# A two-layer attention block on one Trainium2 core: the values of a pair of heads move one slot later, next to another pair's scores

## The chip, the cores and the metric

The kernel runs on one core of one Trainium2 chip. Its engines have their own instruction streams, synchronised by semaphores: TensorE (PE in the rows, PEld for its weight loads), VectorE (DVE), ScalarE (ACT), GpSimd (POOL) and SyncE (SP), which issues the weight loads from memory. The metric is the device time in microseconds, median of the runs; lower is better. All times are microseconds unless marked ns.

## The reference, cut to what matters

Two layers, 256 tokens, width 1024, everything in float32. Each layer has three attention branches of 8 heads, a gated merge of them, and a feed-forward part.

```
z = x @ w_in; (c_q, c_kv, ..., gate_logit) = split(z)
o_mla = softmax(causal(q @ k.T * scale)) @ v               # q, k: 64 + 32 = 96 wide
o_fox = softmax(causal(q @ k.T * scale + decay)) @ v       # 64 wide
o_dsa = softmax(top-64 of the indexer(q @ k.T * scale - slope * dist)) @ v   # 64 wide
gates  = sigmoid(gate_logit + b_gate)                      # 3 x 1024 a token
merged = sum over branches of gates * (o_branch @ w_branch)
x = layernorm(ALPHA * x + merged @ w_out)
x = layernorm(ALPHA * x + (gelu(conv(x @ w_up[gate])) * (x @ w_up[value])) @ w_down)
```

## The kernel before, in words

**Products.** Every product with a weight matrix is done in three matmuls on rounded parts: high x high, high x low, low x high (`product`, L628 to L630). ScalarE makes the high part of each weight panel of 128 x 2048 (`split_hi`, L1105), VectorE the low part (`split_lo`, L1434). Six raw panels and four high parts are in memory at once, so a split waits until the panel four before it was used (`panel_used`).

**Slots.** The 24 heads are 12 pairs: pairs 0 to 3 are FOX, 4 to 7 MLA, 8 to 11 DSA. The attention runs in slots s = 0 to LAST_SLOT, on every engine in an order written out by hand. In each of the first 24 slots TensorE runs one gate tile (`gate_tile`: 24 matmuls of 128 x 256, a tile of `gate_logit`). From slot 24 on it runs the branch projections instead (`branch_panel(q)`: four tiles of 12 matmuls; the first two ahead of the attention work of the slot, the last two behind it). Tiles are counted here from 0: tile u is tile u % 4 of panel u // 4. They go to three PSUM banks in turn, so tile u waits until VectorE has merged tile u - 3. Panel 4 is the first that reads the outputs of DSA, and waits for the low half of pair 11's output.

**One pair i**, before: scores in slot 2i+1 (`scores`, L913: for each of two token tiles two heads, 128 and 256 keys wide); row minima on VectorE in slot 2i+2 (`row_least`, L1566 and L1578) and exponentials on ScalarE (`softmax_exp`, L1179); normalising in slot 2i+3 on VectorE (`normalise`, L1585 and L1590) and, on TensorE, the transposes of the probabilities (`turn_probs`, L925). In slot 2i+4 VectorE copies the even head's (`probs_even_out`, L1596), ScalarE the odd head's (`probs_odd_out`, L1186), and TensorE runs the values (`values`, L942). In slot 2i+5 ScalarE takes the high half of the output out of PSUM (`outputs_hi`, L1191) and VectorE the low half (`outputs_lo`, L1602). There is one PSUM bank for the outputs and one buffer `pts` for the turned probabilities. `even_slot_pair(s, lag)` gives the pair whose lag fits slot s.

**Shapes on TensorE.** FOX and DSA scores use 64 rows of the array, the two heads side by side; MLA scores use 96 rows. Values use 64 columns for each of the two heads, side by side. Everything else near them is 128 x 128, or 128 x 96 for the transposes of MLA's heads (`head_operands`, L892 and L893).

**Merges.** Behind slot 23 VectorE multiplies each branch tile with its gate (`merge`, L1620), and GpSimd adds them up (L1931). In slot 24 `row_least` of pair 11 runs on VectorE ahead of the first merge.

Of the kernel before, what the change touches and what calls it, by code (L numbers as in the profile page):

```python
# [28 lines left out]
NT = T // P  # L29
# [35 lines left out]
OUT_AT = BR_AT + 2 * NB  # L65
# [14 lines left out]
SLOTS = NB * H  # L80
# [4 lines left out]
W_BRANCH = (1, 0, 2)  # L85


LAG_S, LAG_E, LAG_T, LAG_V = 1, 2, 3, 4
LAST_SLOT = 2 * (PAIRS - 1) + LAG_V
HEAD_ROWS = (HD, QK, HD)  # L90

# [46 lines left out]
def build_program(nc, x, positions, w_in, b_gate, b_forget, q_norm, kv_norm, w_uq, w_ukv, w_branch, w_out,  # L138
                  ln1_g, ln1_b, w_up, conv_w, conv_b, w_down, ln2_g, ln2_b, out):
    ctx = ExitStack()  # L140
    with ctx:
# [306 lines left out]
        def even_slot_pair(s, lag):  # L448

            i, odd = divmod(s - lag, 2)  # L450
            return [i] if not odd and 0 <= i < PAIRS else []
# [173 lines left out]
        def _(pe):  # L625
# [270 lines left out]
            def scores(l, i):  # L896

                b, j = divmod(i, 4)
                if i > 0:
                    pe.wait_ge(s_maxima_ready, at("maxima_ready", l, 2 * i))  # L900
                else:
                    pe.wait_ge(s_index_relu_ready, at("index_relu_ready", l, NT))
                if b == MLA:
                    pe.wait_ge(s_head_ready, at("head_ready", l, 2 * j + 2))
                for t in range(NT):
                    for a in range(2):
                        if b == MLA:
                            q, k = qks[0:QK, a, 0, :], qks[0:QK, a, 1, :]
                        elif b == FOX:
                            q, k = spread_rows(fq_t, a)[:, j, :], spread_rows(fk_t, a)[:, j, :]  # L910
                        else:
                            q, k = spread_rows(sq_t, a)[:, j, :], spread_rows(sk_t, a)
                        ins = pe.matmul(ps[:, B_S[a], SPAN[t]], q[:, P * t:P * t + P], k[:, 0:P * (t + 1)],  # L913
                                        start=True, stop=True)
                ins.then_inc(s_scores_ready, 1)
# [12 lines left out]
            def values(l, i):  # L928

                b, j = divmod(i, 4)  # L930
                pe.wait_ge(s_turned_even_ready, at("turned_even_ready", l, i + 1))
                pe.wait_ge(s_turned_odd_ready, at("turned_odd_ready", l, i + 1))
                if i > 0:
                    pe.wait_ge(s_outputs_lo_ready, at("outputs_lo_ready", l, i))
                for c, cols in ((0, slice(0, T)), (1, slice(T, 3 * P))):
                    for a in range(2):
                        h = 2 * j + a
                        if b == DSA:
                            v = z1[:, c, Z_SV:Z_SV + HD]
                        else:  # L940
                            v = (fv, v_tok)[b][:, c, HD * h:HD * h + HD]
                        ins = pe.matmul(ps[HD * a:HD * a + HD, B_O, P * c:T], v, pts[:, a, cols], start=c == 0, stop=c == 1)  # L942
                ins.then_inc(s_pair_output, 1)

            def branch_panel(l, q, tiles=range(4)):

                n, c = divmod(q, 2)
                whi, wlo = panel(l, BR_AT + q, 4, 512)
                if c == 0 and 0 in tiles:

                    pe.wait_ge(s_outputs_lo_ready, at("outputs_lo_ready", l, 4 * (n + 1)))
                for jj in tiles:
                    u = 8 * n + 4 * c + jj
                    if u < 2:
                        pe.wait_ge(s_gate_ready, at("gate_ready", l, SLOTS - 1 + u))
                    if u >= len(B_PROJ):

                        pe.wait_ge(s_proj_gated, at("proj_gated", l, u - len(B_PROJ) + 1))
                    dst = proj_psum(u)
                    for k in range(4):  # L960
                        cols = slice(P * jj, P * jj + P)
                        ins = product(dst, whi[:, k, cols], wlo[:, k, cols], *outputs(4 * n + k), k == 0, k == 3)
                    if jj < 3:
                        ins.then_inc(s_proj_product, 1)
                    else:
                        ins.then_inc(s_panel_used, 1)
# [46 lines left out]
            for l in range(DEPTH):  # L1013
# [37 lines left out]
                for s in range(LAST_SLOT + 1):  # L1051
                    if s < SLOTS:
                        gate_tile(l, s)
                    if H - 1 <= s < 2 * H - 1:
                        head_operands(l, s - H + 1)
                    if SLOTS <= s:
                        branch_panel(l, s - SLOTS, (0, 1))
                    for i in even_slot_pair(s, LAG_S):
                        scores(l, i)
                    for i in even_slot_pair(s, LAG_T):  # L1060
                        turn_probs(l, i)
                    for i in even_slot_pair(s, LAG_V):
                        values(l, i)
                    if SLOTS <= s:
                        branch_panel(l, s - SLOTS, (2, 3))
                for q in range(LAST_SLOT - SLOTS + 1, 2 * NB):
# [29 lines left out]
        def _(act):  # L1096
# [160 lines left out]
            for l in range(DEPTH):  # L1257
# [103 lines left out]
                    if SLOTS <= s:  # L1361
                        split_hi(l, BR_AT + s - SLOTS + 3)
                outputs_hi(l, PAIRS - 1)
                split_hi(l, OUT_AT)
                split_hi(l, OUT_AT + 1)
                merged_hi(l, 0)
                merged_hi(l, 1)
# [59 lines left out]
        def _(dve):  # L1427
# [296 lines left out]
            for l in range(DEPTH):  # L1724
# [66 lines left out]
                for s in range(LAST_SLOT + 1):  # L1791
                    for i in even_slot_pair(s, LAG_T + 1):
                        if i < PAIRS - 1:
                            probs_even_out(l, i)
                    for i in even_slot_pair(s, LAG_E):
                        row_least(l, i)
                    if s % 2 == 0 and s < SLOTS:
                        split_lo(l, GATE_AT + s // 2 + 2)
                    for i in even_slot_pair(s, LAG_E + 1):
                        if i < PAIRS - 1:  # L1800
                            normalise(l, i)
                    for i in even_slot_pair(s, LAG_V + 1):
                        outputs_lo(l, i)
                    if s == SLOTS:
                        merge(l, 0, (0, 1, 2))
                        normalise(l, PAIRS - 1)
                        merge(l, 0, (3,))
                    if s == SLOTS + 1:
                        merge(l, 1, (0, 1))
                        probs_even_out(l, PAIRS - 1)  # L1810
                        merge(l, 1, (2, 3))
                    if s == SLOTS + 2:
                        merge(l, 2)
                    if SLOTS - 1 <= s:
                        split_lo(l, BR_AT + s - SLOTS + 3)
                    if 2 <= s < 18:
                        take_eight(l, s - 2)
                    if s == 17:
                        selection(l)
                outputs_lo(l, PAIRS - 1)  # L1820
                merge(l, 3, (0, 1))
                split_lo(l, OUT_AT)
                merge(l, 3, (2, 3))
                merge(l, 4, (0, 1))
                split_lo(l, OUT_AT + 1)
# [125 lines left out]
```

## Time and profile before

| | |
|---|---|
| time, median of 3 runs | 870.39 us (870.2 to 870.74) |
| profiled execution, its own time | 869.66 us |
| its span | 867.9 us |
| TensorE busy | 850.6 us, 98% |
| VectorE, ScalarE, GpSimd busy | 70%, 54%, 11% |
| attention slots of layer 0, layer 1 | about 87 to 207 us, 512 to 632 us |

A row's start is counted from the start of the span. TensorE's matmuls are pipelined: one lasts about 0.28 us in the rows and the next starts 0.12 us after it, so what a matmul costs is read from start to start. The profile records a float32 matmul, such as those of scores and values, as two, so that the four of a block stand as x8.

### The profile page before, as it was taken

The numbers are of one execution on the slowest core, as the hardware profiler recorded it, in microseconds if no ns is written. First come the engines' busy times: TensorE is split into PE (matmuls) and PEld (weight loads), VectorE is DVE, ScalarE is ACT, GpSimd is POOL, SyncE is SP. The second block draws the span as 40 slices with busy tenths as digits, with TensorE's granted clock in tenths as the row PEclk, the third lists the DMA queues.
The fourth block names the chain that finished last, engine by engine and source line by source line (L and its number), as shares of the span: only waits on it lengthen the run. The fifth ranks groups of instructions, "written<-read, shape, count | busy, mean of one in ns | idle before, by whom it ended". The sixth has DMA issues, their size and how long they took to land.

```text
span 867.9 us, 15821 instructions
## 1 busy us (share of the span) xinstructions
PE 850.6 (98%) x6364; PEld 790.9 (91%) x6364; DVE 609.8 (70%) x1111; ACT 469.4 (54%) x726; POOL 94.3 (11%) x112
## 2 busy tenths in 40 slices
PE   6999999999999999999999999999999999999996
PEld 6899999989999999988889999998898999999885
DVE  5775777877786877665666558778778777666554
ACT  5556867554355555553437477675544465554430
POOL 1003800003500000000000055000071000000000
PEclk9999999999999999999999999999999999999998
DMA  9756443334677666465846664434366776664731
GB/s 305 215 171 210 147 146 99 117 127 148 193 194 198 191 195 194 159 213 180 266 120 166 186 203 133 141 104 125 119 193 179 194 212 187 185 188 135 242 132 48
DMA packets 176407, 148.86 MB, mean 172 GB/s; under 512 B 18156, under 2 KB 149840, under 8 KB 176336
## 3 DMA queue, kind: packets, MB, share of 16 engines
q1 hardware_dynamic: 171712, 143.08, 55.1%
q10 hardware_dynamic: 4624, 4.78, 1.9%
q8 instruction: 50, 0.82, 0.4%
q14 instruction: 21, 0.17, 0.1%
HBM read 146.53 MB, written 1.05 MB: 170 GB/s over the span
## 4 chain that ended last, share of the span: by engine, by line
PE 94%; DVE 2%; ACT 1%; DVEq 1%; DMA 1%; issue 0%; SPq 0%; ACTq 0%
PE ps L628 29%; PE ps L629 28%; PE ps L630 28%; PE ps L913 3%; PE ps L942 2%; PE ps L925 2%; PE ps L686 1%; ACT w_hi L1105 1%; DVEq L1569 1%; DMA raw<-w_in 1%; DVE w_lo L1434 1%; PE ps L892 0%; PE ps L861 0%; PE ps L893 0%; PE ps L879 0%
## 5 line engine op out<-in xcount | busy, mean ns | idle before, releaser
L1434 DVE TENSOR_TENSOR w_lo<-raw,w_hi 128x2048 fp32r<-128x2048 f32 (+3 forms) x142 | 304.0, 2143 | 116.7 <-ACT w_hi L1105 116.6
L628 PE MATMUL ps<-xt_hi,w_hi 128*128 128x256 f32 x1232 | 349.3, 284 | 0.4 <-ACT fq_t L1130 0.4
L629 PE MATMUL ps<-xt_lo,w_hi 128*128 128x256 f32 x1232 | 343.8, 279 | 0.0
L630 PE MATMUL ps<-xt_hi,w_lo 128*128 128x256 f32 x1232 | 343.6, 279 | 0.0
L1105 ACT ACTIVATE w_hi<-raw 128x2048 fp32r<-128x2048 f32 (+3 forms) x142 | 252.8, 1785 | 76.1 <-PE ps L630 70.1
L628 PEld LDWEIGHTS ps<-xt_hi,w_hi 128*128 128x128 f32 x1232 | 231.6, 188 | 5.7 <-issue 4.3
L629 PEld LDWEIGHTS ps<-xt_lo,w_hi 128*128 128x128 f32 x1232 | 231.7, 188 | 0.1
L630 PEld LDWEIGHTS ps<-xt_hi,w_lo 128*128 128x128 f32 x1232 | 231.6, 188 | 0.0
L628 PE MATMUL ps<-w_hi,ht_hi 128*128 128x512 f32 x176 | 68.6, 390 | 0.0
L630 PE MATMUL ps<-w_hi,ht_lo 128*128 128x512 f32 x176 | 68.5, 389 | 0.0
L1215 ACT ACTIVATE cv<-ps,vec_t 128x256 f32<-128x256 f32 x44 | 20.8, 473 | 88.2 <-PE ps L630 84.3
L629 PE MATMUL ps<-w_lo,ht_hi 128*128 128x512 f32 x176 | 68.5, 389 | 0.0
L1931 POOL TENSOR_TENSOR merged<-merged,gated 128x256 f32<-128x256 f32 x32 | 39.6, 1264 | 204.1 <-DVE gated L1620 203.8
L1179 ACT ACTIVATE prob<-prob,least 128x128 f32<-128x128 f32 x96 | 42.8, 447 | 21.3 <-DVE least L1578 21.3
L628 PE MATMUL ps<-w_hi,xt_hi 128*128 128x256 f32 (+2 forms) x144 | 46.4, 322 | 3.4 <-DVE w_lo L1732 2.0
L1668 DVE SCALAR_TENSOR_TENSOR cv<-ps,vec_t,cv 128x255 f32<-128x255 f32 x44 | 21.2, 481 | 36.3 <-ACT cv L1215 36.3
L629 PE MATMUL ps<-w_lo,xt_hi 128*128 128x256 f32 (+2 forms) x144 | 45.4, 315 | 0.0
L630 PE MATMUL ps<-w_hi,xt_lo 128*128 128x256 f32 (+2 forms) x144 | 45.4, 315 | 0.0
L629 PEld LDWEIGHTS ps<-w_lo,ht_hi 128*128 128x128 f32 x176 | 33.0, 188 | 6.8
L628 PEld LDWEIGHTS ps<-w_hi,ht_hi 128*128 128x128 f32 x176 | 33.0, 188 | 6.8
L630 PEld LDWEIGHTS ps<-w_hi,ht_lo 128*128 128x128 f32 x176 | 33.0, 188 | 6.8
L628 PE MATMUL ps<-ot_hi,w_hi 128*128 128x256 f32 x128 | 36.7, 287 | 0.9 <-DVE merged L1620 0.9
(226 smaller groups left out, 1248.7 us busy)
## 6 DMA issues: line engine op xcount, KB each, us to landing
raw<-ffn_w_up SPq DMA_DIRECT2D x88, 512.0 KB, 5.2
raw<-w_in SPq DMA_DIRECT2D x84, 512.0 KB, 4.8
raw<-ffn_w_down SPq DMA_DIRECT2D x32, 512.0 KB, 4.1
raw<-w_branch SPq DMA_DIRECT2D x24, 512.0 KB, 4.6
raw<-w_out SPq DMA_DIRECT2D x16, 512.0 KB, 4.3
raw<-ffn_w_down SPq DMA_DIRECT2D x24, 256.0 KB, 3.0
ln_g<-ln_g ACTq DMA_DIRECT2D x4, 512.0 KB, 3.6
ln_b<-ln_b ACTq DMA_DIRECT2D x4, 512.0 KB, 5.3
```

What stands on the lines that cost most here:

```text
L628: pe.matmul(dst, a_hi, b_hi, start=first, stop=False)
L629: pe.matmul(dst, a_hi, b_lo, start=False, stop=False)
L630: return pe.matmul(dst, a_lo, b_hi, start=False, stop=last)
L913: ins = pe.matmul(ps[:, B_S[a], SPAN[t]], q[:, P * t:P * t + P], k[:, 0:P * (t + 1)], start=True, stop=True)
L925: ins = pe.transpose(ps[:, B_PT[a], P * c:P * c + P], prob[:, i % 2, a, P * c:P * c + P], ident[:])
L942: ins = pe.matmul(ps[HD * a:HD * a + HD, B_O, P * c:T], v, pts[:, a, cols], start=c == 0, stop=c == 1)
L1105: ins = act.activation(panel_hi(l, p)[0:n, cols], panel_raw(l, p)[0:n, cols], ACT.Copy)
L1179: ins = act.activation(p, p, ACT.Exp, scale=-1.0, bias=least[:, i % 2, a, t:t + 1], accum_out=rsum[:, i % 2, a, t:t + 1])
L1215: act.activation(cv[:, buf, :], ps[:, B_UP[f % len(B_UP)], 0:T], ACT.Copy, scale=column(vec_t, V_CW + 2 * FT, f)).then_inc(s_conv_first_ta ...
L1434: ins = dve.tensor_tensor(panel_lo(l, p)[0:n, cols], panel_raw(l, p)[0:n, cols], panel_hi(l, p)[0:n, cols].bitcast(F32), ALU.subtract)
L1668: dve.scalar_tensor_tensor(cv[:, buf, 1:T], ps[:, B_UP[f % len(B_UP)], 0:T - 1], column(vec_t, V_CW + FT, f), cv[:, buf, 1:T], ALU.mult, A ...
L1931: pool.tensor_tensor(merged[:, u % KD, :], merged[:, u % KD, :], gated[:, u % NGATED, :], ALU.add).then_inc(s_merged_added, 1)
```

## The change

`LAG_V` goes from 4 to 5: the values of pair i run in slot 2i+5, and its outputs are taken out in slot 2i+6. Within a slot of TensorE the values move from behind `turn_probs` to ahead of `scores`. In the scores the token tile with 256 keys runs first. There is one slot more (LAST_SLOT 27), so one split and one half merge move from behind the loop into it.

```
-LAG_S, LAG_E, LAG_T, LAG_V = 1, 2, 3, 4
+LAG_S, LAG_E, LAG_T, LAG_V = 1, 2, 3, 5
...
-                for t in range(NT):
+                for t in reversed(range(NT)):
                     for a in range(2):
...
                         branch_panel(l, s - SLOTS, (0, 1))
+                    for i in even_slot_pair(s, LAG_V):
+                        values(l, i)
                     for i in even_slot_pair(s, LAG_S):
                         scores(l, i)
                     for i in even_slot_pair(s, LAG_T):
                         turn_probs(l, i)
-                    for i in even_slot_pair(s, LAG_V):
-                        values(l, i)
                     if SLOTS <= s:
                         branch_panel(l, s - SLOTS, (2, 3))
...
                 outputs_hi(l, PAIRS - 1)
-                split_hi(l, OUT_AT)
                 split_hi(l, OUT_AT + 1)
...
+                    if s == SLOTS + 3:
+                        merge(l, 3, (0, 1))
                     if SLOTS - 1 <= s:
                         split_lo(l, BR_AT + s - SLOTS + 3)
...
                 outputs_lo(l, PAIRS - 1)
-                merge(l, 3, (0, 1))
-                split_lo(l, OUT_AT)
                 merge(l, 3, (2, 3))
```

TensorE, before, at the end of gate tile 22 with the values of pair 9 behind it, and at the end of gate tile 23 with the scores of pair 11 and the transposes of pair 10 (`z1` is the tile that holds DSA's values):

```order
L630 MATMUL ps<-xt_hi,w_lo 128x256
L942 MATMUL ps<-pts,z 64x256 x2
L942 MATMUL ps<-pts,z 64x128 x2
L628 MATMUL ps<-xt_hi,w_hi 128x256
...
L630 MATMUL ps<-xt_hi,w_lo 128x256
L913 MATMUL ps<-sk_t,sq_t 128x128 x2
L913 MATMUL ps<-sk_t,sq_t 128x256 x2
L925 MATMUL ps<-ident,prob 128x128 x6
L628 MATMUL ps<-ot_hi,w_hi 128x256
```

The same place now:

```order
L630 MATMUL ps<-xt_hi,w_lo 128x256
L942 MATMUL ps<-pts,z 64x256 x2
L942 MATMUL ps<-pts,z 64x128 x2
L913 MATMUL ps<-sk_t,sq_t 128x256 x2
L913 MATMUL ps<-sk_t,sq_t 128x128 x2
L925 MATMUL ps<-ident,prob 128x128 x6
L628 MATMUL ps<-ot_hi,w_hi 128x256
```

The values stand behind gate tile 23 now, with no gate tile between them and the scores, and the 256-wide scores are first.

VectorE, before, in slots 24 and 25, from the end of the row minima of pair 11 (L1578) over the merges (L1620) to the copy of pair 11's probabilities:

```order
L1578 ISA prob,least<-prob,selm 128x256
L1578 ISA least 128x1
L1620 SCALAR_TENSOR_TENSOR merged<-gates_early,ps 128x256 x3
L1585 RECIPROCAL rinv<-rsum 128x4
...
L1620 SCALAR_TENSOR_TENSOR merged<-gates_early,ps 128x256
L1434 TENSOR_TENSOR w_lo<-raw,w_hi 128x2048
L1602 TENSOR_TENSOR ot_lo_last<-ps,ot_hi_last 128x256
L1620 SCALAR_TENSOR_TENSOR merged<-gates_late,ps 128x256 x2
L1596 COPY pts<-ps 128x384
```

The same place now (every line number behind L1364 is one lower):

```order
L1577 ISA prob,least<-prob,selm 128x256
L1577 ISA least 128x1
L1601 TENSOR_TENSOR ot_lo_last<-ps,ot_hi_last 128x256
L1619 SCALAR_TENSOR_TENSOR merged<-gates_early,ps 128x256 x3
L1584 RECIPROCAL rinv<-rsum 128x4
...
L1619 SCALAR_TENSOR_TENSOR merged<-gates_early,ps 128x256
L1433 TENSOR_TENSOR w_lo<-raw,w_hi 128x2048
L1619 SCALAR_TENSOR_TENSOR merged<-gates_late,ps 128x256 x2
L1595 COPY pts<-ps 128x384
```

The low half of an output (of pair 9) stands between the row minima and the first merge; before, pair 9's stood in slot 23, and the one shown above is pair 10's.

ScalarE, now, from the copy of the odd head of pair 10 over the four exponentials of pair 11 in slot 24:

```order
L1186 ACTIVATE pts<-ps 128x384
L1179 ACTIVATE prob,rsum<-prob,least 128x128
L1179 ACTIVATE prob,rsum<-prob,least 128x256
L1179 ACTIVATE prob,rsum<-prob,least 128x128
L1179 ACTIVATE prob,rsum<-prob,least 128x256
L1191 ACTIVATE ot_hi_last<-ps 128x256
L1105 ACTIVATE w_hi<-raw 128x2048 x2
```

The high half of pair 9's output (L1191) stands behind the exponentials; before, it stood in slot 23, ahead of the last gate.

## Rows read from the trace of the kernel before

**Rows 1.** The page: TensorE's and others' busy time; granted clock in 40 slices

```profile
PE 850.6 (98%) x6364; PEld 790.9 (91%) x6364; DVE 609.8 (70%) x1111; ACT 469.4 (54%) x726; POOL 94.3 (11%) x112
...
PEclk9999999999999999999999999999999999999998
```

**Rows 2.** Timeline of TensorE, slots 3 to 5: start, duration, engine, line, what [idle before]

```profile
99.41 0.28 PE L630 MATMUL ps<-xt_hi,w_lo 128*128 128x256 f32 x1
99.61 0.93 PE L913 MATMUL ps<-fk_t,fq_t 64*128 64x128 f32 x8
100.47 0.88 PE L925 MATMUL ps<-ident,prob 128*128 128x128 f32 x6
...
103.88 0.27 PE L630 MATMUL ps<-xt_hi,w_lo 128*128 128x256 f32 x1
104.08 0.87 PE L942 MATMUL ps<-pts,fv 128*64 128x256 f32 x8
104.88 0.38 PE L628 MATMUL ps<-xt_hi,w_hi 128*128 128x256 f32 x1
105.11 0.28 PE L629 MATMUL ps<-xt_lo,w_hi 128*128 128x256 f32 x1
105.22 0.28 PE L630 MATMUL ps<-xt_hi,w_lo 128*128 128x256 f32 x1
```

**Rows 3.** Timeline of TensorE, slot 9, scores of the first MLA pair

```profile
125.54 0.27 PE L893 MATMUL ps<-ident,k_tok 128*96 128x128 f32 x1
125.65 1.48 PE L913 MATMUL ps<-qks 96*128 96x128 f32 x8
126.96 0.82 PE L925 MATMUL ps<-ident,prob 128*128 128x128 f32 x6
```

**Rows 4.** Timeline of TensorE, slot 24 of layer 0: tiles 1, 2 and 3

```profile
191.32 0.28 PE L630 MATMUL ps<-ot_hi,w_lo 128*128 128x256 f32 x1
192.29 0.87 PE L942 MATMUL ps<-pts,z 128*64 128x256 f32 x8 [0.69 <-DVE pts L1596]
...
194.48 0.28 PE L630 MATMUL ps<-ot_hi,w_lo 128*128 128x256 f32 x1
195.26 0.38 PE L628 MATMUL ps<-ot_hi,w_hi 128*128 128x256 f32 x1 [0.50 <-DVE merged L1620]
```

**Rows 5.** Timeline of VectorE, slots 23 and 24 of layer 0

```profile
189.48 2.29 DVE L1434 TENSOR_TENSOR w_lo<-raw,w_hi 128x2048 fp32r<-128x2048 f32 x1 [2.41 <-ACT w_hi L1105]
191.68 0.55 DVE L1596 COPY pts<-ps 128x384 f32<-128x384 f32 x1
...
194.78 1.08 DVE L1620 SCALAR_TENSOR_TENSOR merged<-gates_early,ps 128x256 f32<-128x256 f32 x3
```

**Rows 6.** Timeline of ScalarE, slots 23 and 24 of layer 0

```profile
187.17 0.47 ACT L1163 ACTIVATE gates_late<-ps,bg 128x256 f32<-128x256 f32 x1 [2.16 <-PE ps L630]
...
195.65 0.19 ACT L1179 ACTIVATION_READ_ACCUMULATOR prob<-prob,least 128x1 f32 x1
195.74 1.90 ACT L1105 ACTIVATE w_hi<-raw 128x2048 fp32r<-128x2048 f32 x1
197.54 0.36 ACT L1191 ACTIVATE ot_hi_last<-ps 128x256 fp32r<-128x256 f32 x1
```

**Rows 7.** Timeline of VectorE, slot 19: low half of an output, behind pair 8's normalising

```profile
170.33 0.42 DVE L1602 TENSOR_TENSOR ot_lo<-ps,ot_hi 128x256 fp32r<-128x256 f32 x1
```

**Rows 8.** Timeline of TensorE, slot 19: first transpose of pair 8

```profile
171.37 0.33 PE L925 MATMUL ps<-ident,prob 128*128 128x128 f32 x1
```

**Rows 9.** Timeline of VectorE behind slot 26: a split while GpSimd adds

```profile
213.37 2.71 DVE L1434 TENSOR_TENSOR w_lo<-raw,w_hi 128x2048 fp32r<-128x2048 f32 x1
```

**Rows 10.** Timeline at the end: TensorE's last matmul

```profile
860.09 0.39 PE L630 MATMUL ps<-w_hi,ht_lo 128*128 128x512 f32 x1
```

**Rows 11.** Windows: stretch, its length, busy time (x) by engine, granted clock, DMA, GB/s

```profile
861.00:863.30 2.30, 0.00 (x0) 0.00 (x0) 1.98 (x6) 0.29 (x1) 0.00 (x0) 1.00 0.00 0
863.40:867.90 4.50, 0.00 (x0) 0.00 (x0) 2.01 (x3) 0.00 (x0) 0.00 (x0) 0.50 0.31 117
```

More of the change, by code:

```diff
@@ L85 @@
 W_BRANCH = (1, 0, 2)
-LAG_S, LAG_E, LAG_T, LAG_V = 1, 2, 3, 4
+LAG_S, LAG_E, LAG_T, LAG_V = 1, 2, 3, 5
 LAST_SLOT = 2 * (PAIRS - 1) + LAG_V
@@ L904, in scores @@
                     pe.wait_ge(s_head_ready, at("head_ready", l, 2 * j + 2))
-                for t in range(NT):
+                for t in reversed(range(NT)):
                     for a in range(2):
@@ L1057, in _ @@
                         branch_panel(l, s - SLOTS, (0, 1))
+                    for i in even_slot_pair(s, LAG_V):
+                        values(l, i)
                     for i in even_slot_pair(s, LAG_S):
@@ L1061, in _ @@
                         turn_probs(l, i)
-                    for i in even_slot_pair(s, LAG_V):
-                        values(l, i)
                     if SLOTS <= s:
@@ L1363, in _ @@
                 outputs_hi(l, PAIRS - 1)
-                split_hi(l, OUT_AT)
                 split_hi(l, OUT_AT + 1)
@@ L1813, in _ @@
                         merge(l, 2)
+                    if s == SLOTS + 3:
+                        merge(l, 3, (0, 1))
                     if SLOTS - 1 <= s:
@@ L1820, in _ @@
                 outputs_lo(l, PAIRS - 1)
-                merge(l, 3, (0, 1))
-                split_lo(l, OUT_AT)
                 merge(l, 3, (2, 3))
```

## Prediction

> **What bounds the kernel now.** I read the page's busy table first: TensorE is busy for 98% of the span and the clock row shows 9 in every slice but the last [rows 1]. Nothing can be gained here that doesn't shorten TensorE's own row of work or one of its waits, and any wait that is added is paid in full. Then I read TensorE's timeline over one pair of heads, and the chain of waits for the places where it stood still. In the slots of the attention there are none: for both layers TensorE's starts follow each other without a wait from the first scores to the end of slot 23. What is left there is the price of going from one kind of matmul to another.
>
> That price is read from start to start. Inside a gate tile matmuls start every 0.12 us (105.11 to 105.22). The first scores start 0.20 behind the last gate matmul (99.41 to 99.61), the first values too (103.88 to 104.08), and the first gate matmul behind the values takes 0.23 until the next may start (104.88 to 105.11) [rows 2]. So a gate tile that stands behind values and ahead of scores pays about 0.085 at its end and 0.11 at its start. The scores' block is 0.86 long and the values' 0.80. MLA's scores use 96 rows; they start 0.11 behind the transpose ahead of them and take 1.31 (125.65 to 126.96): no switch is paid [rows 3].
>
> The other place is slot 24, where branch tiles take the place of the gate tiles. TensorE waits there twice: the values of pair 10 wait for the copy of the turned probabilities on VectorE (0.69), and the fourth branch tile (tile 3; only three banks serve them) waits 0.50 for VectorE's first merge [rows 4]. Both hang on one chain: the end of gate tile 23 frees the last gate on ScalarE (187.17) [rows 6], behind it the split of a weight panel there, then VectorE's half of it (189.48), the copy (191.68), the row minima of pair 11 and the first merge at 194.78 [rows 5]. TensorE's tile 3 starts at 195.26.
>
> **The change part by part.** *Main slots.* Values of pair i now run in slot 2i+5, directly ahead of the scores of pair i+2. Where these are 64-row scores the gate tile between the two blocks is gone from this place, and with it one entry (0.085) and one exit (0.11): 0.195 saved. Entering the scores from the values is a switch that the trace doesn't show. Its bounds: nothing at all, which adds the scores' own entry and exposed start, about 0.2 more per place; or as dear as the two switches it replaces, which saves 0. I take the nearest rows, one entry of the 0.20 kind, so 0.195. There are six such places a layer (scores 2, 3 of FOX and 8 to 11 of DSA). For the four of MLA the values leave to a 128-row kind of matmul as before, only another one: 0. Sum: 6 x 0.195 = 1.17 us a layer.
>
> The trace shows that leaving and entering 64-row or 64-column work costs about 0.1 at each edge [rows 2]. The Trainium skill (TensorEngine Tiling (Array Packing), section Key Properties) says that changing the tiling mode, not only the tile, drains TensorE. Values to scores is 128x64 to 64x128, a change of mode, so by that rule the edge stays and 0.195 is right; a reader who took both for "small tiles" would expect 0.4. No run here shows that edge yet.
>
> *Order inside the scores.* The 256-wide pair of matmuls now comes first. Streaming is the same. Bounds: the values' block, which runs wide first, is 0.80 against 0.86 for the same columns, so up to 0.055 saved at 16 blocks, 0.9 us in all; or nothing, because what is exposed at a block's head is the first weight load and the values load 64 columns against 128 [rows 2]. I take 0, since MLA's blocks show that the widths alone cost nothing: their 1.31 us is what four 128-wide and four 256-wide pieces stream, with no start exposed [rows 3].
>
> *VectorE and ScalarE in the main slots.* The eviction of the values (0.36 and 0.42) moves from the odd slot behind the normalising to the even slot ahead of it. VectorE then normalises 0.42 later and TensorE asks 0.195 sooner. The tightest pair where this applies is pair 8: normalised at 170.4, turned at 171.37, 0.95 of slack, of which 0.34 is left [rows 7, 8]. So nothing is paid; without that cover it would be paid pair by pair. ScalarE evicts behind its exponentials, ahead of a gate that TensorE needs only 3 us later. No DMA and no panel changes its order on the queues.
>
> *Slot 24.* Gate tile 23 now ends earlier against the start of slot 24, because the values of pair 9 (0.80) stand behind it; the whole chain above comes 0.80 earlier. But VectorE's first merge now has a new instruction ahead of it, the low half of pair 9's output, and that waits for the high half on ScalarE, which is queued behind all four exponentials of pair 11. Those end at 195.84 [rows 6], while the merge began at 194.78. So the merge comes behind 195.84, plus 0.36 [rows 6] less the 0.10 by which ScalarE's instructions overlap, plus a hand-over of 0.03, plus 0.42 [rows 7] less 0.09 of overlap, at about 196.45: 1.67 later. Queued behind it on VectorE are all merges, and TensorE's tile 3 waits for the first. Net: 1.67 - 0.80 = 0.87 later against the start of slot 24, so tile 3 starts at about 196.13 on the old scale.
>
> *Cover lost.* Before, the values of pair 10 ran inside that very wait, in front of tile 2, and cost nothing. Now they run in slot 25 at full price: entry 0.09, block 0.80, and something between 0 and 0.11 at the transposes behind them; I take 0.05. Sum 0.94. TensorE meanwhile stands still from the end of tile 2 (191.32 [rows 4] and its twelve matmuls at 0.117, the last 0.28 long: about 193.0) to 196.13, 3.1 us in one piece.
>
> *Slot 27.* The values of pair 11 now end one half panel, two tiles or 2.8 us, before the branch panel that needs all pairs; formerly it was ten tiles. Their low half stands on VectorE behind a panel's split (2.29, or 2.71 when GpSimd gets in between [rows 9]). Following VectorE from slot 24 I find it ready 0 to 0.5 us before TensorE asks. Cost 0; if it is late, up to 0.65 a layer.
>
> *Sum.* Per layer -1.17 + 0.87 + 0.94 = +0.64, two layers +1.3 us. The profiled execution took 869.66 us (span 867.9), 0.7 below the median of the runs, so it would take 871.0, and the median 870.4 becomes 871.7, +0.15%. A measurement of this kernel can tell 0.2%, 1.74 us, from no change; this is just inside it.
>
> **The rivals.** *The tail is free.* If the eviction of pair 9 didn't hold up the merges, only the saving would be left: -2.3, and with the waits of slot 24 (0.69 + 0.50) closed up to -4.7: 865.7 to 868.1. For it: values no longer wait for the copy. Against: the order of ScalarE's and VectorE's rows in slot 24, which leaves no way round. Chance 0.10, faster.
>
> *The clock falls in the new gap.* At the end of the program TensorE's last matmul starts at 860.09 and ends at 860.48, and the granted clock, 1.00 until 863.3, is 0.50 (1.2 GHz) from 863.4: 2.9 us of idleness were enough there [rows 10, 11]. The new gap in slot 24 is 3.1 us. Against it: the gaps of up to 1.3 us passed without a fall, and nothing says that the same idleness always brings one. If it falls, everything behind the gap runs at half rate until it is granted again; the half-rate stretch that the rows show is 4.5 us, which would lose about 2.2 us a layer: 873.9 with one fall, 876.2 with two. It decides as soon as the gap passes about 3 us. The Trainium skill (TensorE: Matmul & The Clock Gate, Part 1) calls half rate the default that activity releases, which fits this; it gives no other sum. Chance 0.15, slower.
>
> *The change saves nothing in the main slots.* Values to scores costs both edges (+2.3 against my sum), or slot 27's low half is late (up to +0.65 a layer): 872.4 to 875.3. For it: VectorE's slack in slot 27 is thinner than my reading error. Against: one drain should serve for both. Chance 0.17, slower for 0.14 of it.
>
> *The edge is free.* Another 0.2 at twelve places: 869.3, no measurable change. Chance 0.03.
>
> **How the numbers follow.** My own case has 0.55; its sum is 0.4 us from the limit of 872.1, and its terms are good to about 0.6, so 0.13 of it lies above: slower. Same: 0.42 + 0.03 + 0.03 = 0.48. Slower: 0.13 + 0.15 + 0.14 = 0.42. Faster: 0.10. The range 869.3 to 874.2 takes in the free edge, the dear edge and one fall of the clock, and leaves out the free tail and two falls.
>
> **What would show it right or wrong.** In TensorE's timeline values to scores start to start 0.80, then scores 0.86 to 0.85, and the even slots' gate tiles entered at 0.12. The waits list should lose the wait of the values for the copy and show one of about 3.1 us a layer, tile 3 behind VectorE's first merge, with a low-half subtraction ahead of it on VectorE that waits for ScalarE. I am wrong if that wait is under 1 us, if the clock row drops near 195 or 620 us, or if the transposes wait for normalising.

## The result, and the profile after

The changed kernel takes 875.12 us (median of 9 runs, 872.48 to 877.5) against 870.39 us (869.35 to 871.26): a ratio of 1.0057, 95% interval 1.0044 to 1.0069. It is slower, and it lies above the predicted range. The profiled execution took 874.82 us with a span of 873.1, 5.2 us more than before's 867.9. Two executions in a slow state, one of e6_split_only (1051.5 us, mean granted clock 0.752) and one of the kernel before beside e5 to e8 (1706.41 us), are left out of every median and ratio here.

The page first: TensorE has the same 6364 matmuls as in [rows 1] and 1.5 us more busy time. The clock row is as it was; a stretch of some 3 us doesn't show in slices of 22 us.

```profile
PE 852.1 (98%) x6364; PEld 797.1 (91%) x6364; DVE 610.1 (70%) x1111; ACT 466.3 (53%) x726; POOL 94.6 (11%) x112
...
PEclk9999999999999999999999999999999999999998
```

The waits of TensorE: who waited, for whom, us in all, how often, the longest. First two of the kernel before:

```profile
PE ps L942 <- DVE pts L1596: 1.4, 2, 0.7
PE ps L628 <- DVE merged L1620: 0.9, 2, 0.5
```

And of the changed kernel:

```profile
PE ps L628 <- DVE merged L1619: 6.3, 2, 3.2
...
PE ps L942 <- DVE ot_lo L1601: 0.6, 2, 0.3
```

The wait for the first merge has grown from 0.9 to 6.3 us, and the wait for the copy of the probabilities is gone; both were forecast. The wait of the values for an output's low half is new and was not.

TensorE's timeline of the changed kernel at four places: start, duration, line, what, and in brackets the idle time ahead with what ended it.

```profile
107.39 0.27 PE L630 MATMUL ps<-xt_hi,w_lo 128*128 128x256 f32 x1
107.59 0.87 PE L942 MATMUL ps<-pts,fv 128*64 128x256 f32 x8
108.39 0.92 PE L913 MATMUL ps<-fk_t,fq_t 64*128 64x256 f32 x8
109.25 0.87 PE L925 MATMUL ps<-ident,prob 128*128 128x128 f32 x6
...
169.53 0.28 PE L630 MATMUL ps<-xt_hi,w_lo 128*128 128x256 f32 x1
170.13 0.87 PE L942 MATMUL ps<-pts,v_tok 128*64 128x256 f32 x8 [0.32 <-DVE ot_lo L1601]
...
192.75 0.28 PE L630 MATMUL ps<-ot_hi,w_lo 128*128 128x256 f32 x1
196.23 0.58 PE L628 MATMUL ps<-ot_hi,w_hi 128*128 128x256 f32 x1 [3.20 <-DVE merged L1619]
...
197.04 0.41 PE L628 MATMUL ps<-ot_hi,w_hi 128*128 128x256 f32 x1
197.25 0.41 PE L629 MATMUL ps<-ot_lo,w_hi 128*128 128x256 f32 x1
...
199.76 0.28 PE L630 MATMUL ps<-ot_hi,w_lo 128*128 128x256 f32 x1
199.87 0.28 PE L628 MATMUL ps<-ot_hi,w_hi 128*128 128x256 f32 x1
```

The first block answers [rows 2]: entry 0.20 (107.39 to 107.59), values 0.80, scores 0.86. From values to scores there is no gate tile and no free edge. The second is a wait that before doesn't have: the values of pair 7 start 0.60 behind the last gate matmul instead of 0.20, for the low half of an output. The third answers [rows 4]: TensorE stands still ahead of tile 3 from about 193.0 to 196.23. The fourth shows what follows: matmuls 0.21 apart, where [rows 2] has 0.12, until 199.4.

The windows of the changed kernel confirm that this is the clock (columns as in [rows 11]): 1.00 all through the idle time, 0.50 as work begins again, 1.00 from 199.5.

```profile
192.90:195.90 3.00, 0.13 (x2) 0.00 (x0) 1.56 (x8) 2.70 (x10) 0.00 (x0) 1.00 0.00 0
196.00:199.30 3.30, 3.07 (x14) 3.07 (x15) 2.04 (x9) 1.14 (x2) 0.00 (x0) 0.50 0.01 2
199.50:202.00 2.50, 2.50 (x23) 2.43 (x21) 2.50 (x3) 1.67 (x1) 0.00 (x0) 1.00 0.56 147
```

VectorE's timeline of the changed kernel at the two waits. At 169.57 the low half of pair 6 stands behind a weight split; TensorE's values of pair 7 write the bank that it reads. In slot 24 the row minima are done at 194.0, but the first merge has to wait for the low half of pair 9, and that for ScalarE: [rows 5] had the merge at 194.78.

```profile
167.36 2.29 DVE L1433 TENSOR_TENSOR w_lo<-raw,w_hi 128x2048 fp32r<-128x2048 f32 x1
169.57 0.42 DVE L1601 TENSOR_TENSOR ot_lo<-ps,ot_hi 128x256 fp32r<-128x256 f32 x1
...
193.93 0.08 DVE L1577 DVE_READ_ACCUMULATOR2_ANT least<- 128x1 f32 x1
195.32 0.43 DVE L1601 TENSOR_TENSOR ot_lo_last<-ps,ot_hi_last 128x256 fp32r<-128x256 f32 x1 [1.32 <-ACT ot_hi_last L1191]
195.76 1.08 DVE L1619 SCALAR_TENSOR_TENSOR merged<-gates_early,ps 128x256 f32<-128x256 f32 x3
```

ScalarE's timeline there: the high half is queued behind the last exponential of pair 11, as in the prediction. [rows 6] is the same chain, 0.80 later and with the high half behind the weight split.

```profile
194.84 0.18 ACT L1179 ACTIVATION_READ_ACCUMULATOR prob<-prob,least 128x1 f32 x1
194.93 0.36 ACT L1191 ACTIVATE ot_hi_last<-ps 128x256 fp32r<-128x256 f32 x1
195.20 1.90 ACT L1105 ACTIVATE w_hi<-raw 128x2048 fp32r<-128x2048 f32 x1
```

Where the 5.2 us are, from starts of matmuls that both programs have (layer 0; layer 1 in brackets):

| stretch of TensorE | before | after | difference | predicted |
|---|---|---|---|---|
| span's start to first index matmul | 79.63 | 80.34 | +0.71 | 0 |
| first scores to transposes of pair 10 | 94.96 (94.96) | 94.24 (94.29) | -0.71 (-0.66) | -1.17 |
| from there to the transposes behind the attention | 54.91 (54.84) | 58.49 (57.10) | +3.58 (+2.26) | +1.81 |
| all else | | | 0.0 | 0 |

The first line is no effect of the change: nothing is different up to there, and over all the profiled executions here that start lies between 78.9 and 80.5. It goes with the clock's record: in the five executions with 78.9 to 79.6 the first record of full rate starts at 6.1 to 6.7 us, in the nine with 80.2 to 80.5 at 10.5 to 12.0. So I compare profiles by the span behind it: 788.29 before, 792.74 after.

### The profile page after: what moved, and what is told of

Its sections match the earlier page's. It is cut to its first block, busy times and chain, and to the rows that moved or that the text cites. A ratio compares the mean times of both kernels' runs of the same rounds, so it can differ in the third digit from the quotient of the medians.

```text
span 873.1 us, 15823 instructions
## 1 busy us (share of the span) xinstructions
PE 852.1 (98%) x6364; PEld 797.1 (91%) x6364; DVE 610.1 (70%) x1111; ACT 466.3 (53%) x726; POOL 94.6 (11%) x112
## 4 chain that ended last, share of the span: by engine, by line
PE 91%; DVE 5%; DVEq 1%; ACT 1%; issue 1%; POOL 0%; ACTq 0%; POOLq 0%
PE ps L628 28%; PE ps L630 27%; PE ps L629 27%; PE ps L913 3%; PE ps L942 2%; PE ps L925 2%; DVE w_lo L1433 2%; PE ps L686 1%; DVE prob L1577 1%; DVEq L1568 1%; ACT w_hi L1105 1%; DVE prob L1565 0%; PE ps L892 0%; PE ps L893 0%; PE ps L861 0%
```

## The experiments

"Rest" is the span of the profiled execution behind the first index matmul. "Gap" is the longest pitch between two matmul starts in slot 24, layer 0 and 1. "Clock" is the mean granted clock of the runs. A pitch is the time from one start to the next. The experiments ran in three groups, each beside new runs of the kernel before, and the ratio is to those: their medians were 870.61 beside e1 to e4, 870.54 beside e5 to e8 and 869.86 beside e9 to e12, so medians of different groups can differ by 0.75 us for no other reason.

| kernel | median us | ratio to before | 95% | rest us | gap us | clock |
|---|---|---|---|---|---|---|
| before | 870.39 | | | 788.29 | 0.97, 0.97 | 0.997 to 0.998 |
| after | 875.12 | 1.0057 | 1.0044 to 1.0069 | 792.74 | 3.48, 3.41 | 0.991 to 0.997 |
| e1_t_only | 870.66 | 1.0001 | 0.9992 to 1.001 | 788.77 | as before | 0.997 to 0.998 |
| e8_lag_only | 874.42 | 1.0046 | 1.0033 to 1.0059 | 791.48 | 3.48, 3.38 | 0.995 to 0.997 |
| e2_filler | 873.98 | 1.0037 | 1.0024 to 1.0049 | 791.44 | none | 0.997 to 0.998 |
| e3_lo_late | 869.84 | 0.9986 | 0.9977 to 0.9995 | 787.73 | 1.68, 1.65 | 0.998 |
| e5_early_out | 871.5 | 1.0013 | 1.0004 to 1.0022 | 788.35 | 2.07, 2.01 | 0.994 to 0.998 |
| e10_bank_only | 875.24 | 1.006 | 1.0045 to 1.0075 | 792.42 | 3.51, 3.38 | 0.992 to 0.996 |
| e9_both_lo | 869.11 | 0.9991 | 0.9982 to 0.9999 | 787.25 | 1.68, 1.68 | 0.998 to 0.999 |
| e12_long_gap | 881.57 | 1.013 | 1.0117 to 1.0143 | 798.78 | 5.83, 5.79 | 0.990 to 0.992 |
| e6_split_only | 869.55 | 0.9989 | 0.998 to 0.9999 | 787.80 | slot 25: 1.09 | 0.997 to 0.998 |
| e4_mixed | 866.87 | 0.9958 | 0.9946 to 0.9971 | 785.43 | 0.69, 0.63 | 0.997 |
| e7_mixed_split | 867.84 | 0.997 | 0.9958 to 0.9982 | 785.48 | slot 25: 1.10 | 0.997 to 0.999 |
| e11_mixed_shift | 872.44 | 1.0028 | 1.0016 to 1.0039 | 789.08 | tile 17: 2.70 | 0.993 to 0.997 |

### The two halves of the change: e1_t_only and e8_lag_only

The kernel before with the new order of token tiles, and the changed kernel with the old order:

```
-                for t in range(NT):
+                for t in reversed(range(NT)):
```

> The kernel before with one edit: in the scores the token tile with 256 keys runs first. My theory: nothing, 870.4 +- 0.3; the block of 64-row scores stays within 0.01 us of 0.86 and MLA's of 1.31. Rival A (the wide-first order shortens each 64-row block by 0.055): 869.5. Rival B (this order is part of what made the changed kernel slower): 871 to 872.

> The changed kernel with the old order of the token tiles in the scores. My theory: the slot is what counts, the order is nothing, so 875.1 +- 1, clock falls included. Rival 'the wide tile first makes up for something at the edge from values to scores': 876 or more, and a block from values to scores longer than 0.80.

The order alone leaves the time as it is (1.0001), and without it the shift is as slow as the whole change: 874.42, inside the spread of the nine runs of the changed kernel. All of the effect is the shift of the values. The profile of e8 had no fall of the clock in either gap, and its rest is 3.2 us above before's: that is what the change costs without the clock: the waits and the lost cover, less what the main slots save.

### The gap filled: e2_filler

The changed kernel with 56 small matmuls between tiles 2 and 3 of slot 24, whose product nobody reads:

```
+                    if s == SLOTS:
+                        branch_panel(l, 0, (2,))
+                        pe.wait_ge(s_turned_even_ready, at("turned_even_ready", l, PAIRS - 1))
+                        keep_clock_up(B_PT[0], 56)
+                        branch_panel(l, 0, (3,))
```

> The changed kernel, with 56 matmuls of 128x128 on an identity (bf16, results not used) between tile 2 and tile 3 of slot 24 in each layer, in the time in which TensorE otherwise waits for the first merge. The wait itself is not shortened. Theory 'the clock falls in the gap': the granted clock stays 1.00 behind both gaps, and the median goes down by about one fall, 1.4 to 1.7 us, to 873.3 to 873.7, with a smaller spread over the runs. Rival 'the loss beyond my forecast is all waits and the clock is chance': no change, 875.1.

TensorE works through the wait, the median is just above the range that I expected, and the stretch in which the changed kernel had half rate is at full rate (windows of e2_filler):

```profile
190.00:194.00 4.00, 4.00 (x55) 3.96 (x54) 2.96 (x14) 1.77 (x7) 0.00 (x0) 1.00 0.05 18
194.00:198.00 4.00, 3.81 (x45) 3.67 (x43) 3.41 (x11) 3.03 (x5) 0.00 (x0) 1.00 0.01 2
```

The waiting itself stays. The rest is 791.44, as in e8, where the clock did not fall either, and the median 1.1 us under the changed kernel's. So the clock is 1.1 us of the 4.7 in the median. Taken against the runs of before beside each, the filled gap costs 3.4 us and the clock 1.4; the profiled executions say the same, 3.2 us of rest without a fall and 1.3 more with one.

### The gap shortened: e3_lo_late

VectorE's low half of pair 9 behind the first three merges of slot 24, in the changed kernel:

```
-                        outputs_lo(l, i)
+                        if s != SLOTS:
+                            outputs_lo(l, i)
                     if s == SLOTS:
                         merge(l, 0, (0, 1, 2))
+                        outputs_lo(l, SLOTS // 2 - LAG_V // 2 - 1)
```

> The changed kernel with one instruction of VectorE moved: in slot 24 the low half of pair 9's output stands behind the first three merges, not ahead of them. Theory 'the merges queue behind it': tile 3 starts 1.67 us sooner in each layer, the gap falls from 3.2 to 1.5 us, the clock no longer falls there: -3.3 - 1.5, about 870.3. If only the wait counts and the clock would fall anyway: 871.8. Rival 'the merges are late for another reason (the exponentials on ScalarE or the split of the panel)': 875, no change.

One instruction moved behind three merges takes 5.3 us off, the clock's share among them, and puts the kernel under before. The pitch falls from 3.48 to 1.68, and none of its 11 runs has a clock under 0.998. Its waits:

```profile
PE ps L628 <- DVE merged L1619: 2.8, 2, 1.4
...
PE ps L942 <- DVE ot_lo L1601: 0.6, 2, 0.3
```

### Outputs first everywhere: e5_early_out

In the changed kernel both halves of an output ahead of the slot's exponentials and row minima:

```
+                    for i in even_slot_pair(s, LAG_V + 1):
+                        outputs_lo(l, i)
                     for i in even_slot_pair(s, LAG_E):
                         row_least(l, i)
```

> The changed kernel with each output taken out of PSUM at the head of its slot: the high half ahead of the exponentials on ScalarE, the low half ahead of the row minima on VectorE. Theory 'one bank for the outputs': the wait of pair 7's values (0.39 a layer) for pair 6's low half is gone; in slot 24 the merges are 1.67 - 0.33 sooner, so the gap is 1.8 to 2.1 us and the clock holds: -0.8 - 2.7 against the changed kernel and less its falls, 869.5 to 870. Rival 'pair 7's values wait for something else, as VectorE's selection work': that wait stays at 0.39 and the time is 870.5.

It is slower than the 869.5 to 870 that I expected. The wait of pair 7 goes and the gap is as long as I said, but the clock did not hold as I said it would. Slot 24's pitch is 2.07, where e3 has 1.68: the low half (191.25) now costs its 0.34 ahead of the row minima, and the merge comes at 194.21. Six of its 11 runs have a clock of 0.995 or 0.994; those of e3 and e9, with 1.68, have none in 22.

```profile
191.25 0.41 DVE L1601 TENSOR_TENSOR ot_lo_last<-ps,ot_hi_last 128x256 fp32r<-128x256 f32 x1
...
194.21 1.08 DVE L1619 SCALAR_TENSOR_TENSOR merged<-gates_early,ps 128x256 f32<-128x256 f32 x3
```

### The missed wait by itself: e10_bank_only and e9_both_lo

The same, but only in slots under 24 (e10), and that together with e3's edit (e9):

```
+                    if s < SLOTS:
+                        for i in even_slot_pair(s, LAG_V + 1):
+                            outputs_lo(l, i)
                     for i in even_slot_pair(s, LAG_E):
                         row_least(l, i)
```

> The changed kernel with only the first of those edits: outputs taken out first in slots below 24, slot 24 untouched. Theory: the output-bank wait of pair 7 goes (0.60 to 0.20 us in both layers), slot 24 keeps its pitch of 3.4 to 3.5 us and the clock's falls come as often as in the changed kernel: 875.12 less 0.8, so 874.3 us. Rival (the wait of pair 7 hides another behind it, so that the time only moves): 875.1 us.

> The changed kernel with two edits on VectorE and ScalarE: in slots below 24 the outputs of a pair are taken out first (high half ahead of the exps, low half ahead of the row minima and the weight split), and in slot 24 the low half of pair 9 stands behind the first three merges. Theory (the missed output-bank wait costs 0.39 us a layer, and the short gap of slot 24 stays as it was where only that low half was moved): the pitch of 0.60 us ahead of the values of pair 7 becomes 0.20, the pitch of slot 24 stays near 1.68, the clock stays at full rate through it; against the kernel with only the second edit (869.84 us) 0.8 us less, so 869.1 us. Rival (the earlier outputs on ScalarE and VectorE make exps and row minima of the next pair late by as much): the 0.60 goes and other pitches of the same size come, 869.8 or above.

The low half of pair 6 moves from 169.57 to 165.26 and the values of pair 7 start 0.20 behind the gate tile (timelines of VectorE and of TensorE in e10_bank_only):

```profile
165.26 0.41 DVE L1605 TENSOR_TENSOR ot_lo<-ps,ot_hi 128x256 fp32r<-128x256 f32 x1
...
168.17 2.28 DVE L1437 TENSOR_TENSOR w_lo<-raw,w_hi 128x2048 fp32r<-128x2048 f32 x1
170.38 0.17 DVE L1588 RECIPROCAL rinv<-rsum 128x4 f32<-128x4 f32 x1
170.62 1.01 DVE L1593 TENSOR_SCALAR prob<-prob,rinv 128x128 f32<-128x128 f32 x4
```

```profile
169.35 0.28 PE L630 MATMUL ps<-xt_hi,w_lo 128*128 128x256 f32 x1
169.56 0.87 PE L942 MATMUL ps<-pts,v_tok 128*64 128x256 f32 x8
170.36 0.92 PE L913 MATMUL ps<-sk_t,sq_t 64*128 64x256 f32 x8
171.32 0.41 PE L925 MATMUL ps<-ident,prob 128*128 128x128 f32 x2
```

Of the 0.39 us only 0.24 to 0.30 a layer come back. The transposes of pair 8 follow right on the scores, 0.39 us sooner than they did, while VectorE normalises later (170.62, behind the split), and start 0.96 behind the scores' first matmul, 0.10 more than in [rows 2]. That is the rival of both expectations, in part. In the median e10 can't be told from the changed kernel (875.24), where I expected 874.3; in the profiles the main slots are 0.5 us shorter over both layers, in e10 against the changed kernel and in e9 against e3. e9 has both waits mended and the clock at 0.998 or more. Its 869.11 is the expected number, but by luck: its runs of before were 0.75 us lower than e3's, and against them its ratio is no better than e3's (0.9991 and 0.9986, intervals overlapping).

### The gap lengthened: e12_long_gap

Six instructions on VectorE ahead of the low half of pair 9, in the changed kernel:

```
+                    if s == SLOTS:
+                        for n in range(6):
+                            dve.drain()
+                            dve.tensor_tensor(selm[:], selm[:], selm[:], ALU.max)
```

> The changed kernel with six more VectorE instructions (128x384 maxima of a mask with itself, about 0.56 us each by the row of the same shape, 3.3 us together) ahead of pair 9's low half in slot 24: TensorE's gap there grows from a pitch of 3.4 to one of about 6.8 us. Theory (TensorE's idle time is what lets the granted clock fall, by chance at 3.4 us): at 6.8 us it falls in both layers, in every run: 875.12 + 2 x 3.3 + up to 1.4 for the layer that did not fall in the profile, 881.7 to 883.1 us, granted clock mean 0.993 or below in all runs. Rival (the fall has another cause, such as what runs elsewhere on the chip, and the gap's length does not matter): one fall or none as in the changed kernel, 881.7 us, and runs with a mean of 0.997 among them.

The pitch grew to 5.83 and not to 6.8: a part of the six ran in the 1.32 us in which VectorE had waited for ScalarE. Now both layers fall, and in layer 0 the clock is down while TensorE still waits (windows of e12_long_gap):

```profile
194.00:196.00 2.00, 0.00 (x0) 0.00 (x0) 1.77 (x4) 1.99 (x2) 0.00 (x0) 0.50 0.01 4
...
200.00:201.00 1.00, 1.00 (x7) 1.00 (x7) 0.60 (x2) 0.54 (x1) 0.00 (x0) 0.65 0.00 0
...
626.00:628.00 2.00, 0.21 (x1) 0.21 (x2) 1.93 (x6) 0.34 (x1) 0.00 (x0) 0.84 0.00 0
628.00:630.00 2.00, 2.00 (x10) 2.00 (x11) 1.49 (x7) 0.00 (x0) 0.00 (x0) 0.50 0.00 0
```

All four runs have 0.990 to 0.992, as the theory asked; the median, 881.57, is just under its range. The gaps are 2.35 longer, twice, 4.7 us; measured is 6.5 over the changed kernel, which leaves 1.8 for the clock. In the profiles the rest is 6.0 longer, which leaves 1.3 for the second fall. The rival, another cause than TensorE's own idleness, doesn't fit: no fall with 1.0 or 1.68 us, signs of one in some runs with 2.07, in 18 of 20 with 3.4 to 3.5, in all with 5.8.

### Without the shift: e6_split_only

What holds slot 24 up in the kernel before is a chain with a weight split in it [rows 5]. Here before's split of branch panel 2 goes behind the first merges:

```
-                    if SLOTS - 1 <= s:
+                    if s == SLOTS:
+                        split_lo(l, BR_AT + 2)
+                    if SLOTS <= s:
                         split_lo(l, BR_AT + s - SLOTS + 3)
```

> The kernel before with one instruction of VectorE moved: the low half of branch panel 2 behind the first merges of slot 24 instead of in slot 23. Theory (slot 24 is bound by VectorE's order, in both kernels): both waits of slot 24 (0.77 and 0.66 a layer by starts) go, 2.8 us in all, 867.6. Rival 'ScalarE's split or the copy of the odd head is next behind it': half of it, 869.2.

My expectation was too high a gain: the interval of the ratio, 0.998 to 0.9999, allows 0.1 to 1.7 us. Both waits of slot 24 go, but two splits now stand in a row and the low half and merges of slot 25 behind them (timelines of VectorE and TensorE in e6_split_only):

```profile
195.50 4.48 DVE L1434 TENSOR_TENSOR w_lo<-raw,w_hi 128x2048 fp32r<-128x2048 f32 x2
199.90 0.41 DVE L1602 TENSOR_TENSOR ot_lo_last<-ps,ot_hi_last 128x256 fp32r<-128x256 f32 x1
```

```profile
200.70 0.39 PE L628 MATMUL ps<-ot_hi,w_hi 128*128 128x256 f32 x1 [0.81 <-DVE merged L1620]
```

### Both orders mixed: e4_mixed, e7_mixed_split, e11_mixed_shift

The values of pairs 0 to 9 one slot later, as in the change, those of 10 and 11 where they were, ahead of the gate or branch tile; outputs taken out first in their slot; old order of scores. The core of the edit:

```
+        def values_of(s, late):
+            return [i for i in range(PAIRS) if (i < LATE) == late and s == 2 * i + LAG_V + late]
...
-                    for i in even_slot_pair(s, LAG_V):
+                    for i in values_of(s, True):
                         values(l, i)
+                    for i in values_of(s, False):
+                        values(l, i)
```

> Values of pairs 0 to 9 as in the changed kernel, those of pairs 10 and 11 in their old slots; outputs are taken out at the head of their slot, ahead of exponentials and row minima; the scores' order as before the change. Theory (edges save 1.17 us a layer; the cover of pair 10's values and the early merge come back, about 1.0 more a layer): 866.1, clock without a fall. Rival 'the switches save less than 0.1 each and the gain in the slots is chance': 868.5 or above. Rival 'taking outputs out early delays the exponentials': TensorE waits for normalising, over 870.

This beats both kernels: 866.87 us, 0.9958 of before. It has the main slots' saving without the long gap. The values of pair 10 run inside slot 24's wait again. Pair 9's low half stands ahead of the row minima and the merges, as in e5, but no longer waits for ScalarE; now the values of pair 10 wait for it (timeline of VectorE in e4_mixed, and TensorE's two waits there):

```profile
189.68 0.41 DVE L1613 TENSOR_TENSOR ot_lo_last<-ps,ot_hi_last 128x256 fp32r<-128x256 f32 x1
...
192.65 1.08 DVE L1631 SCALAR_TENSOR_TENSOR merged<-gates_early,ps 128x256 f32<-128x256 f32 x3
```

```profile
190.24 0.87 PE L951 MATMUL ps<-pts,z 128*64 128x256 f32 x8 [0.29 <-DVE ot_lo_last L1613]
193.12 0.39 PE L637 MATMUL ps<-ot_hi,w_hi 128*128 128x256 f32 x1 [0.41 <-DVE merged L1631]
```

The early outputs cost 0.16 a layer at the transposes of pair 8, which start 1.02 behind the scores instead of 0.86. The three edits of e4 were not taken apart.

e7 adds e6's edit to it, e11 moves all four branch splits one slot later (`split_lo(l, BR_AT + s - SLOTS + 2)`, and panel 5's behind slot 26).

> The mixed kernel (values of pairs 0 to 9 directly ahead of scores, 10 and 11 in their old slots, outputs taken out early) with the split of branch panel 2 moved on VectorE as well. Theory: what slot 24 still waits (0.4 + 0.5 a layer) goes too, 866.9 - 1.8 = 865.1. Rival 'the tail is then bound by something later (the merged sums on GpSimd)': 866.5 or above.

> The mixed kernel (values of pairs 0 to 9 in the new slots, 10 and 11 in the old ones) with VectorE's low splits of the branch panels 2 to 5 each one slot later, so that no two of them stand in a row in slot 24. Theory: with the split of panel 2 behind slot 24's merges, and none behind it there, the pitch of 1.10 us that two splits in a row made ahead of slot 25's fourth tile goes, and the two of 0.57 and 0.69 of the mixed kernel stay gone: against 866.87 about 0.9 a layer less than the kernel with two splits in a row (867.84), so 866.1 us, clock at full rate. Rival (the raw panels come free a slot later, so that loads and later splits are late and the wait moves to slots 26 and 27 or to the output projection): 867.5 us or above.

e7's rest is e4's (785.48 and 785.43), so my expectation of 1.8 us less failed: it trades the two waits for the one of 1.10 in slot 25. The rival had the time, but what binds is VectorE's two splits in a row and not GpSimd. The intervals of the two ratios overlap. In e11 the pair of splits has only gone elsewhere, and it takes longer there, with GpSimd at work beside it (timelines of VectorE and TensorE in e11_mixed_shift). The rival was right: the wait moved, to tile 17, the second of panel 4, and it is longer than those it replaced.

```profile
211.52 5.46 DVE L1445 TENSOR_TENSOR w_lo<-raw,w_hi 128x2048 fp32r<-128x2048 f32 x2
216.90 0.74 DVE L1631 SCALAR_TENSOR_TENSOR gated<-gates_early,ps 128x256 f32<-128x256 f32 x2
```

```profile
217.37 0.38 PE L637 MATMUL ps<-ot_hi_last,w_hi 128*128 128x256 f32 x1 [2.42 <-DVE gated L1631]
```

## Why the prediction was wrong

The direction of my own case was right, its size was not: I had +1.3 us, the change costs 3.2 without the clock, and the clock comes on top. Of the 3.4 us between 871.7 and 875.12, 0.8 is a wait that I had put at nothing, 1.1 to 1.4 the clock, which I had left among the rivals, and the remainder small sizes, most of them behind slot 23. With the clock kept up (e2, 873.98) the median lies inside the range, near its end; with the clock's falls it lies above.

*Main slots: right.* Between two pairs with 64-row scores the step from one pair's scores to the next falls from 8.27 us to 8.065, and over the eleven steps of a layer the change is -1.10 without the missed wait, against -1.17. The block of values is 0.80 ahead of scores as it was ahead of a gate tile, so neither the free nor the dear edge is true. The Trainium skill's rule that a change of tiling mode drains the engine (TensorEngine Tiling (Array Packing), section Key Properties) agrees with that: the first scores start 0.20 behind the last values matmul.

*Order inside the scores: right.* Nothing, by e1 and e8.

*VectorE and ScalarE in the main slots: this step failed.* I followed one consequence of the moved eviction, that normalising comes later, and found 0.34 us of slack. The other consequence I didn't look at: the outputs of all pairs use one bank, and the next pair's values are due at 169.74, while VectorE reads it until 169.98; formerly a whole slot lay between (in the trace of before, 161.84 to 166.71). Pair 6's low half stands behind the selection's masks, the longer row minima of the first DSA pair and a weight split. It costs 0.39 a layer, 0.8 us in all. The slack that I did work out was real and thin too: once e10 takes the bank's wait away, normalising is late by 0.10.

*Slot 24: right within 0.1.* Tile 3 starts 7.69 us behind the slot's start in layer 0 and 7.58 in layer 1, where the sum gave 7.59; against before's 6.72 and 6.65 that is 0.97 and 0.93, where it gave 0.87. The instruction that the sum put ahead of the merges is there and waits for ScalarE's last exponential, and e3 shows that it alone makes the gap long.

*Cover lost: right.* The values of pair 10 run at full price in slot 25: in layer 1, where the clock did not fall, tile 6 starts 5.84 behind tile 3 and before 4.89, so 0.95, where the sum gave 0.94.

*Slot 27: a size inside its bound.* I took 0 with up to 0.65. (The cover that I gave for before, ten tiles, was misread: from pair 11's values at 205.93 to panel 4 at 215.24 it is six.) In layer 1 two matmuls that read the last outputs start 0.195 apart instead of 0.117 twice over, 0.16 in sum, and two in the output projection 0.30 and 0.34 apart instead of 0.227, another 0.18. These and about 0.1 of small starts make +2.26 from +1.81. The pair in the output projection is no effect of the shift: in the profiles of e1 and e6, which don't have it, two matmuls there start 0.37 to 0.39 and 0.34 apart in layer 1 too. No experiment took the others apart.

*The rival of the clock: right mechanism, wrong chance and price; it should have been in the sum.* The sign that I had named, the clock dropping near 195 us, is there, at 195.99. I gave it 0.15, since nothing in the trace of before had a gap of that length but the end of the program. It was in fact the one row that bore on the question, and it showed a fall after 2.9 us; against it stood only gaps of 1.3 us or less, which say nothing on 3.1. Nor was 2.9 a limit: over all the profiles the fall came from 2.0 to 5.1 us after the end of TensorE's last matmul, so a gap of 3.2 us of idleness brings it in some runs and in some layers only. Eight of the nine runs have a clock under 0.997. The price of one fall is 1.43 and not 2.2: the half rate lasted 3.41 us and not 4.5, 0.2 of it still in the gap, and the 36 matmuls of tiles 3 to 5 took 5.83 us instead of 4.40.

So the median is 870.4 + 1.3 predicted + about 0.8 for the bank's wait + 0.1 for the main slots' other steps + 0.9 for slots 24 to 27 + 1.1 for the clock = 874.6, beside 875.12 measured. What remains is within what start-up spreads. The 0.9 is a remainder read from the table and not an effect that an experiment shows: about 0.2 of it is slot 24.

## What to carry to other kernels

When a consumer is moved later, list for its output buffer both neighbours: what now waits ahead of the reader in its engine's queue, and how soon the next writer of the same bank comes; a hand-over that had a whole slot of cover became a wait of 0.4 us here. An instruction that waits for another engine must not stand ahead of merges that free TensorE's banks: one subtraction put behind three merges was worth 5.3 us of 875, some 1.3 of it the clock's. And a new gap of several us on TensorE costs more than itself, since matmuls may run at half rate behind it; split the move, so that the pairs at the end keep their old place inside a wait.

## What the runs showed of the hardware

- The clock's fall depends on how long TensorE is idle, and not sharply: none in 22 runs with 1.68 us between starts, signs of one (a mean of 0.996 or less) in 6 of 11 with 2.07, in 5 of 6 with 2.7 (e11), in 18 of 20 with 3.4 to 3.5 (after, e8, e10), in all 4 with 5.8. In the profiles the granted clock fell 2.0 us after the end of the last matmul at the earliest (e12, layer 0: 191.88 to 193.87) and 5.1 at the latest (layer 1: 622.28 to 627.37); at the end of the programs it was 2.4 to 4.4. What sets that time within these bounds no run here shows. In the profiles the half rate lasted 3.41 us in three of four falls and 6.83 in the one that began while TensorE still had 3.6 us to wait.
- Two 128x2048 splits in a row take 4.48 us on VectorE (e6), and 5.46 where GpSimd's additions run beside them for the first 3.3 us (e11). No run shows that pair without them.
- The first 80 us, in which all kernels here have the same instructions, vary by 1.6 us from one profiled execution to another, and come out short where the full rate is on record from 6.1 to 6.7 us and long where it is from 10.5 to 12.0: a difference of that size between two single profiles is no effect, until it is found behind the start.
